# Sparse branch of a transformer block: choice of keys, head norms, rotations and values in one stage, rotation summed by TensorE

## The reference, cut to what matters

```python
q_a = partial_rope(rms_norm(q_a, g_qn_a), cos_a, sin_a)      # 8 heads of 64
k_a = partial_rope(rms_norm(k_a, g_kn_a), cos_a, sin_a)
q_i = partial_rope(q_i, cos_a, sin_a)                         # 8 index heads of 64
k_i = partial_rope(k_i, cos_a, sin_a)                         # one index key of 64
dots  = einsum('bqhc,bsc->bhqs', q_i, k_i) * IDX_DIM ** -0.5
index = einsum('bhqs,bqh->bqs', relu(dots), w_i * IDX_HEADS ** -0.5)
_, idx = top_k(where(causal, index, NEG), 128)
o_a = softmax(q_a . k_a[idx] / 8) @ v_a[idx]
y   = o_a * silu(z_a)              # then the branch matrix, times sigmoid of gate logits
```

## Time and profile before

| what | us |
|---|---|
| runs | 1928.23, 1931.80, 1931.84; median 1931.8 |
| the profiled execution | 1929.16 |
| its span | 1927.4 |
| PE busy | 1733.2 (90%) |
| DVE busy | 885.3 (46%) |
| ACT busy | 701.9 (36%) |
| POOL busy | 727.8 (38%) |
| mean granted clock of PE | 0.945 |

### The profile page before, as it was taken

The page is one execution under the profiler, slowest core; times in us unless marked ns, Lnnn a source line. Parts: engine busy times, 40 slices in busy tenths (PEclk is TensorE's granted clock), DMA queues, the critical chain, the costliest instruction groups (busy, mean ns, idle before and its releaser), DMA issues. The chain is left out here.

```text
span 1927.4 us, 25419 instructions
## 1 busy us (share of the span) xinstructions
PE 1733.2 (90%) x10328; PEld 1304.2 (68%) x10328; DVE 885.3 (46%) x1462; ACT 701.9 (36%) x1182; POOL 727.8 (38%) x376
## 2 busy tenths in 40 slices
PE   6999968889998999999999987889787789987999
PEld 4866648768785878888788864644574456775777
DVE  5658774447523455333113807956212864313231
ACT  4334442233424432322233322224434255344431
POOL 5423323315540445555444535300323611452242
PEclk9999989989999999999999998969888889998999
DMA  4312110004330223322233420100212010432131
GB/s 168 129 55 60 61 35 24 3 15 147 115 98 22 88 77 102 96 91 94 88 99 98 135 78 22 50 16 6 71 53 73 11 44 12 131 115 72 60 104 55
DMA packets 39572, 138.56 MB, mean 72 GB/s; under 512 B 4384, under 2 KB 5664, under 8 KB 38304
## 3 DMA queue, kind: packets, MB, share of 16 engines
q1 hardware_dynamic: 39456, 136.93, 22.4%
HBM read 132.72 MB, written 4.19 MB: 71 GB/s over the span
## 5 line engine op out<-in xcount | busy, mean ns | idle before, releaser
L352 POOL TENSOR_TENSOR parts<-ring,parts 128x1024 fp32r<-128x1024 f32 (+3 forms) x251 | 571.6, 2281 | 946.6 <-ACT parts L343 946.2
L390 PE MATMUL banks<-h_hi,parts 128*128 128x512 f32 x1096 | 476.7, 435 | 31.2 <-ACT a_gate L570 9.8
L391 PE MATMUL banks<-h_lo,parts 128*128 128x512 f32 x1096 | 439.4, 401 | 0.0
L392 PE MATMUL banks<-h_hi,parts 128*128 128x512 f32 x1096 | 438.9, 400 | 0.0
L343 ACT CAST parts<-ring 128x1024 fp32r<-128x1024 f32 (+3 forms) x251 | 244.8, 979 | 234.2 <-PE banks L392 213.6
L390 PEld LDWEIGHTS banks<-h_hi,parts 128*128 128x128 f32 x1096 | 210.5, 192 | 113.3 <-issue 60.1
L391 PEld LDWEIGHTS banks<-h_lo,parts 128*128 128x128 f32 x1096 | 210.8, 192 | 57.8 <-issue 12.8
L392 PEld LDWEIGHTS banks<-h_hi,parts 128*128 128x128 f32 x1096 | 210.6, 192 | 49.9
L2617 ACT CAST ffn_act_hi<-ffn_gate 128x512 fp32r<-128x512 f32 x22 | 13.7, 621 | 167.1 <-DVE ffn_gate L2516 167.1
L2573 DVE TENSOR_TENSOR ffn_raw<-banks,ffn_root 128x512 f32<-128x512 f32 x22 | 15.2, 692 | 125.3 <-PE banks L392 125.2
L390 PE MATMUL banks<-ffn_act_hi,parts 128*128 128x512 f32 x176 | 69.8, 396 | 3.2 <-DVE ffn_gate L2516 3.2
(11 more groups left out here) (539 smaller groups left out, 3120.5 us busy)
## 6 DMA issues: line engine op xcount, KB each, us to landing
ring<-weights SPq DMA_DIRECT2D x211, 512.0 KB, 3.5
ring<-weights SPq DMA_DIRECT2D x24, 256.0 KB, 2.6
ring<-weights SPq DMA_DIRECT2D x8, 384.0 KB, 3.1
x<-xT SPq DMA_DIRECT2D x2, 1024.0 KB, 6.0
x<-xT SPq DMA_DIRECT2D x1, 2048.0 KB, 7.8
x_spill<-x SPq DMA_DIRECT2D x2, 1024.0 KB, 4.8
x<-x_spill SPq DMA_DIRECT2D x1, 2048.0 KB, 7.6
outT<-x SPq DMA_DIRECT2D x8, 256.0 KB, 2.0
```

Source lines behind the costliest of these rows:

```text
L352: self.nc.gpsimd.tensor_tensor(self.parts[:, t % PARTS, 1, 0:w], self.ring[:, t % SLOTS, 0:w], self.parts[:, t % PARTS, 0, 0:w].bitcast(F3 ...
L390: nc.tensor.matmul(out, w.hi, x.hi, start=first, stop=False)
L391: nc.tensor.matmul(out, w.hi, x.lo, start=False, stop=False)
L392: return nc.tensor.matmul(out, w.lo, x.hi, start=False, stop=last)
```

## The change

Stages 1 to 5 become one stage, `select_keys`. In the order of the lists:

- PE: spread, rotation of `ki` and the four `qi`, eight sums of squares, dots of the second query block, turn of the means, dots of the third and fourth, turns of the norm factors. Then, after all relus and the four key norms, eight times four steps of the values' product (`fill`) and one rotation, and 36 background steps.
- A rotation is now DVE multiplying the tile by sin and POOL by cos into two buffers each (parts of `y`), PE adding matrix x (x sin) and identity x (x cos) in one bank, and ACT copying the bank back.
- DVE: two sine multiplies, the spread's copy, three more sine multiplies, means, dots with the reciprocal between the first two blocks, key norms, and then the 16 rounds, with a sine multiply after each of the first eight.
- POOL: five cosine multiplies, its squares, and then eight cosine multiplies, every second of them behind the split of one tile.
- The relu buffers and dot banks go from four to three. `CHOOSE_STEPS` goes from 64 to 36, and no background step lies in the rotations.

```diff
-CHOOSE_STEPS = 64
+CHOOSE_STEPS = 36
-def choose_keys(k, qi, ki, wi, chosen, background):
+def select_keys(k, qk, qi, ki, wi, wiT, v, chosen, cos, sin, y, sg, gained_matrix, q_scale, background, fill):
+        norms = Norms(k, ctx, [(AHD, [(qk[:, t, :], qk[:, t, :], P, k.vec("g_qn_a_2" if t < 4 else "g_kn_a_2"))]) for t in range(8)],
+                      S, 2, room=sg, kept=(4, q_scale[:], AHD ** -0.5), sum_bank=3)
+        items = [(x, matrix, cos) for x in (ki[:], *(qi[:, t, :] for t in range(4)))]
+        items += [(qk[:, t, :], gained_matrix, gained_cos) for t in range(4)] + [(qk[:, t, :], matrix, cos) for t in range(4, 8)]
+        FIRST = 5
+        DOTS = 3
+        def pe_rotate(pe, i):
+            pe.wait_ge(*G("sin_taken").ge(i + 1))
+            if i >= 3:
+                pe.wait_ge(*G("rotated").ge(i - 2))
+            bank = k.banks[4 + i % 3]
+            nc.tensor.matmul(bank, m, by_sin[:, i % 2, :], start=True, stop=False)
+            pe.wait_ge(*G("cos_ready").ge(i + 1))
+            nc.tensor.matmul(bank, k.const("ident"), by_cos[:, i % 2, :], start=False, stop=True).then_inc(*G("swapped").inc())
+        def act_rotate(act, i):
+            act.wait_ge(*G("swapped").ge(i + 1))
+            nc.scalar.copy(items[i][0], k.banks[4 + i % 3]).then_inc(*G("rotated").inc())
+        def dve_rotate(dve, i):
+            if i >= 2:
+                dve.wait_ge(*G("swapped").ge(i - 1))
+            nc.vector.tensor_tensor(by_sin[:, i % 2, :], items[i][0], sin, ALU.mult).then_inc(*G("sin_taken").inc())
+        def pool_rotate(pool, i):
+            if i >= 2:
+                pool.wait_ge(*G("swapped").ge(i - 1))
+            if i == FIRST:
+                pool.wait_ge(*G("gains_ready").ge(2))
+            if i == FIRST + 4:
+                pool.wait_ge(*G("normed").ge(4))
+            nc.gpsimd.tensor_tensor(by_cos[:, i % 2, :], items[i][0], items[i][2], ALU.mult).then_inc(*G("cos_ready").inc())
...
+            def _(pe):
+                for i in range(FIRST):
+                    pe_rotate(pe, i)
+                pe.wait_ge(*G("turned_taken").ge(1))
+                norms.pe_sums(pe)
+                pe.wait_ge(*G("rotated").ge(FIRST))
+                pe_dots(pe, 1)
+                norms.pe_means(pe)
+                pe_dots(pe, 2)
+                pe_dots(pe, 3)
+                norms.pe_turns(pe)
+                pe.wait_ge(*G("relu_ready").ge((ST - 1) * AH))
+                pe.wait_ge(*G("normed").ge(4))
+                for i in range(FIRST, len(items)):
+                    fill.pe(pe, 4)
+                    pe_rotate(pe, i)
+                background.pe(pe, CHOOSE_STEPS)
...
+            def _(act):
+                norms.act_squares(act, None, 0, 4)
+                for i in range(FIRST):
+                    act_rotate(act, i)
+                norms.act_squares(act, None, 4)
+                act_dots(act, 1)
+                norms.act_root(act)
+                act_dots(act, 2)
+                norms.act_wide(act, 0, 2)
+                act_dots(act, 3)
+                norms.act_wide(act, 2, 4)
+                for i in range(FIRST, len(items)):
+                    fill.act(act, 4)
+                    act_rotate(act, i)
+                fill.end_act(act)
+                background.act(act, CHOOSE_STEPS)
...
             def _(dve):
+                for i in range(2):
+                    dve_rotate(dve, i)
+                for i in range(2, FIRST):
+                    dve_rotate(dve, i)
+                norms.dve_means(dve)
+                dve_dots(dve, 1)
+                norms.dve_rstd(dve)
+                dve_dots(dve, 2)
+                dve_dots(dve, 3)
+                norms.dve_parts(dve, 0, 4)
...
+                    if FIRST + r8 < len(items):
+                        if r8 == 0:
+                            dve.wait_ge(*G("normed").ge(4))
+                        dve_rotate(dve, FIRST + r8)
...
             def _(pool):
+                for i in range(FIRST):
+                    pool_rotate(pool, i)
+                norms.pool_squares(pool)
+                for i in range(FIRST, len(items)):
+                    if (i - FIRST) % 2 == 0:
+                        k.split_low(pool, fill.first[0] + (i - FIRST) // 2 + 1 + LEAD)
+                    pool_rotate(pool, i)
                 k.split_low(pool, k.split_h)
...
-                project_tokens(k, "a_v", k.h, S, lambda act, t, b: nc.scalar.copy(v[:, t, :], b))
+                gained_matrix = k.sbuf(start.index, "a_gained_matrix", [P, P])
+                fill = Fill(k, [TokenFill("a_v", k.h, S, range(ST), v)])
                 background = gates(k, "a_z", z, sg)
-                head_norms(k, [(qk[:, t, :], P, 2, AHD, "g_qn_a_2" if t < 4 else "g_kn_a_2") for t in range(8)],
-                           room=sg, kept=(4, q_scale[:], AHD ** -0.5))
-                rotate_tiles(k, [(x, P, k.const("rotate_a"), cos[:], sin[:]) for x in tiles], background,
-                             4, "g_qn_a_2", sg)
-                choose_keys(k, qi, ki, wi[:], chosen, background)
+                select_keys(k, qk, qi, ki, wi[:], wiT, v, chosen, cos[:], sin[:], y, sg, gained_matrix[:], q_scale, background, fill)
```

More of the change, by code:

```diff
@@ L726, in act, with act_squares @@
         self.act_parts(act)
-    def act_squares(self, act, beside=None):
+    def act_squares(self, act, beside=None, begin=0, end=MAX_ROWS):
         k, nc, G, n, nt, per, tiles = self.k, self.k.nc, self.named, self.n, self.nt, self.per, self.tiles
         for i, (g, first, last, src, dst, rows, gain) in enumerate(tiles):
-            if not self.by_pool[i]:
+            if begin <= i < end and not self.by_pool[i]:
                 square, use = self.squares[i][0:2]
@@ L746, in act_roots, with act_wide @@
         cols = len(self.groups) * per
-        means = self.st[:] if self.multi else k.banks[1][:, 0:nt * cols].rearrange("p (j c) -> p j c", c=cols)
+        means = self.st[:] if self.multi else k.banks[self.sum_bank + 1][:, 0:nt * cols].rearrange("p (j c) -> p j c", c=cols)
         nc.scalar.activation(self.st[:], means, ACT.Sqrt).then_inc(*G("root_ready").inc())
-        for g in range(self.plain, len(self.groups)):
+    def act_wide(self, act, begin, end):
+        k, nc, G, n, nt, per, tiles = self.k, self.k.nc, self.named, self.n, self.nt, self.per, self.tiles
+        for g in range(self.plain + begin, self.plain + end):
             rows, m = self.groups[g][1][0][2], g - self.plain
@@ L797, in pe @@
         self.pe_sums(pe)
+        self.pe_means(pe)
         self.pe_turns(pe)
@@ L827, in pe_sums, with pe_means @@
             mm.then_inc(*G("sums_ready").inc())
+    def pe_means(self, pe):
+        k, nc, G = self.k, self.k.nc, self.named
         if not self.multi:
-            cols = len(self.groups) * per
+            cols = len(self.groups) * self.per
             pe.wait_ge(*G("mean_ready").ge(1))
-            for j in range(nt):
-                mm = nc.tensor.transpose(k.banks[1][:, j * cols:(j + 1) * cols], self.sums[:, j * P:(j + 1) * P],
+            for j in range(self.nt):
+                mm = nc.tensor.transpose(k.banks[self.sum_bank + 1][:, j * cols:(j + 1) * cols], self.sums[:, j * P:(j + 1) * P],
                                          k.const("ident", cols)[:, 0:cols])
@@ L2944, in _ @@
             def _(pe):
[L2945 to L2953, removed]
+                for t in range(ST):
+                    last = nc.tensor.matmul(k.banks[3][:, t * AH:(t + 1) * AH], wiT[:, t * P:(t + 1) * P],
+                                            k.const("ident", AH)[:, 0:AH], start=True, stop=True)
+                last.then_inc(*G("rows_spread").inc())
+                for i in range(FIRST):
[13 more added lines that the diff above has]
+                    pe_rotate(pe, i)
                 background.pe(pe, CHOOSE_STEPS)
```

96 lines of the change are left out of this document (55 added, 41 removed).

## The result

The changed kernel took 1936.14 us, the median of 20 runs (1932.75 to 1941.79); the kernel before took 1930.31 beside it (20 runs). The ratio is 1.0031, interval 1.0023 to 1.0039: slower by 0.3%, where 0.8% faster was forecast. The page of the changed kernel gives the span and the busy times, as the earlier trace rows do for the kernel before.

The account below looks back on a forecast made before the run. TensorE, busy for 90% of the span, was taken as the bound. Merged stage 118.5, attention 94, finish 20.1 and branch products 24.1 sum to 256.7 against 272.2 us: 15.5 less, 1916 us, range 1902 to 1929.

Parts of the forecast that it names:

- The merged stage: Sparse branch's product, norms, rotations, dots and choice as one stage: 118.5 us against 143.6, with TensorE setting the end.
- Norms and dots: First part of the merged stage, with first rotations, sums of squares and dots: 43.5 us.
- the eight items: Merged stage's loop, each item four fill steps and a rotation: four plain, three stalled, ending at 86.9 us.
- The three stalls: Loop items 7, 9 and 11: TensorE waits 2.1 us each for a cosine multiply behind POOL's split.
- The finish and the branch products: End of the sparse branch: finish 20.1 us against 7.2 with 28 steps left, products 24.1 against 26.1 at full clock.
- The attention: Sparse attention with 32 background steps instead of 19: 94 us against 95.3, bounds 91 and 108.
- The clock, rule and row: Sparse attention: skill's rule that activity releases the clock gives 1910 us; the trace row disagreed, so clock allowances stayed.
- The allowance of 3 us: Low clock at the sparse attention's start: 94 us taken, where full clock from the start gives 91.
- rival 3: Merged stage's eight-item loop at half clock: 26 us more, kernel slower at 1942 us; chance 0.09.
- Rival 2: Sparse attention stays low as today, two heads at half clock: 108 instead of 94, 1930 us, no change; chance 0.11.
- Rival 1: No stall in the loop, no low clock, attention starts at full clock: 27.8 us less, 1904; chance 0.20.

Follow-up runs that it names:

- run 4: Changed kernel, GpSimd's cosine multiply ahead of its split: 1933.81 us; with ScalarE's early copy of finished background accumulators in the sparse attention as well: 1904.17 us.
- run 3: Sparse attention's score products over all 128 rows instead of 64: 1906.7 us in the changed kernel, 1913.46 us in the kernel before (one run each).
- run 6: Changed kernel with early accumulator copies in merged stage and sparse attention, and 40 instead of 36 background steps in the merged stage: 1905.49 us.
- run 1: ScalarE copies the background accumulator at the job's last step in the sparse attention: changed kernel 1910.02 us, the kernel before with the same edit 1923.61 us.
- run 7: Changed kernel with early copies (latent and memory attentions too), 40 steps, cosine ahead of split, first fill steps ahead of the norms' wait: 1884.50 us.
- run 5: Changed kernel, TensorE does the first four fill steps ahead of its wait for the four key norms: 1933.10 us.

## Why the prediction was wrong

**The merged stage: right.** Forecast 118.5, measured 119.0. Norms and dots ended at 44.3 (43.5), the eight items at 88.7 (86.9). TensorE set the end: VectorE's last threshold starts at 1225.51, 16 us ahead of the stage's end. The three stalls were where they were put, each behind a split, and 2.14, 1.69 and 1.70 instead of 2.1 (the waits' second row; run 4 shows that the split ahead of the cosine product made them). VectorE's multiply beside a split took 2.75, near the 2.82 of the earlier trace rows. The timeline of VectorE and GpSimd there:

```profile
1180.72 2.75 DVE L2988 TENSOR_TENSOR a_y<-x,sin_a 128x512 f32<-128x512 f32 x1
```

```profile
1180.57 2.36 POOL L352 TENSOR_TENSOR parts<-ring,parts 128x1024 fp32r<-128x1024 f32 x1 [13.73 <-ACT parts L343]
```

**The finish and the branch products: right.** 20.2 (20.1; the row's 85 matmuls are the 84 and the next stage's first) and 23.7 at clock 1.00 (24.1).

**The attention: this is the step that failed.** It read "Latent: 84.6 with 32 steps and four drains ... 8 x 1.34 = 10.7 more: 95.3 ... I take 94, bounds 91 ... and 108". Measured 115.1, so 21.1 of the 21.4 us by which the sum missed (278.1 against 256.7) are in this one term. It carried the latent branch's price of a drain into a head whose score products have 64 rows. There a drain of 1.99 us costs 7.2 of the head's time; it is 3.8 with 128 rows, and 2.1 to 3.7 in the latent branch with its 96 (run 3). Without drains and at the full clock the stage takes 81.6 (run 6). So 94 left 12.4 us for drains and low clock, and they took 33.5. The upper bound was too low for the same reason. It let the low clock occur once, at the start, and four drains can bring it four times.

The kernel before showed both prices. It has two drains in this stage. One lies inside the low start: its 2.98 us end at 1276.88, and the low clock lasted to 1296.5. The other is in these rows of its timeline and windows:

```profile
1306.26 0.64 PE L390 MATMUL banks<-h_hi,parts 128*128 128x512 f32 x1 [2.97 <-ACT a_gate L570]
```

```profile
1306.00:1312.00 6.00, 5.74 (x16) 0.72 0.14 46
1312.00:1358.00 46.00, 42.86 (x166) 1.00 0.00 1
```

Behind that wait the clock was 0.72 for 6 us, then 1.00. So one drain was dear and one cheap, and I let 62.4 us at 0.97 speak for all. The height of the scores alone doesn't explain the cheap one: they have 64 rows there too. What differs is that a value product, with 128 rows, starts 1.6 us behind that drain, at 1307.90, where in the changed kernel it stands 12.4 us behind (1280.92 to 1293.27). I argue that from the timelines; no run moved one, and it is not the whole of it, since the clock came back ahead of the value product behind the third drain of the changed kernel (1319.85). The prediction counted the steps that move into the attention (32 for 19), and their four drains only through the latent branch's total. It did not ask what the end of a job costs in this stage: a step at which the bank is full is another thing than a step.

**The clock, rule and row.** The row should have been trusted further than it was. TensorE was busy for 29.50 of 29.50 us at 0.51 (run 1, second fence). The Trainium skill ("TensorE: Matmul & The Clock Gate", "The HAM clock gate") has activity release the clock; this trace disagrees as far as busy time is meant. By that rule, in the prediction's own figures, the attention would have cost 91. The allowance of 3 us that was kept was nearer to the rule's size than to the row's.

**The rivals.** The slower side came true, but not by rival 3: the eight-item loop ran at 0.96, not at half clock. Rival 2 had the place right (the attention's clock) and the trigger wrong. Rival 1, no stall and no low clock, needs both dealt with, and only run 7 has that, among other edits: merged stage 113.5 and attention 81.7, together 195.2, where the rival had 109.2 and 91, together 200.2. Runs 4 (1904.17) and 6 (1905.49) come near its 1904 with one of the two still there each: a low start in the profiled execution of run 4, the stalls in run 6.

**Not settled.** What brings the clock down at this attention's start without a drain. It was low there in the runs without steps, with the cosine first, and with both edits of run 4; it was high in the changed kernel itself and in runs 1, 5, 6 and 7. The waits ahead are the same in size in all of them, 0.77 and 0.93 to 1.08 us; in runs 6 and 7, with 40 steps, the one of 0.77 lies four steps further ahead. Each of these is one profiled execution, and run 4's times with both edits suggest that it can differ between executions of one kernel. Not settled either is why 64-row products keep the clock low for longer.

## What to carry to other kernels

When background work is moved into a latency-bound stage, count the ends of its jobs as well as its steps: at each one an accumulator is drained, and where that copy stands in another engine's program decides whether TensorE waits. A wait of 2 us is priced by what TensorE does behind it, at the clock that it then has, and not by its length; read that price per head, with and without the wait, in the very stage that it goes to. Before a reordering is dropped as slower, move the late copy ahead: here that turned 0.3% slower into 1.0% faster, of which the same copy gives the kernel before 0.4%. With the other edits it was 2.4%, some 8 us of it in branches that the change doesn't touch.

## What the runs showed of the hardware

- A stretch in which TensorE has no gap can stay at 1.2 GHz for some 29 us (run 1, kernel before: busy 29.50 of 29.50 us at a mean of 0.51). With 64-row float32 score products it did; with 128 rows in the same place the low start was over after 5 us (run 3), and behind a drain of 1.99 us the low clock lasted some 3.5 us instead of 10 to 17.
- A wait of 1.99 us, and one of 1.56 (run 1), was followed by the fall to 1.2 GHz within 1.3 us of its end. In run 4 the fall came 1.9 us into a stage, behind a wait of 1.08. A wait need not bring it: behind the 1.85 us that end at 1583.01 in the latent branch of the kernel before the clock stayed at 1.00.
- 64-row scores cost time at the full clock too: 9.88 us a head against 8.51.
- The clock at a stage's start can depend on the schedule of the stage before: with three waits removed there (6.3 us), the next stage was 6.5 us longer, with 28.1 us at 0.51 from near its start (run 4; one profiled execution, the ten times lie within 3.5 us).
